# A down projection by seven block products in a one-core decoder step

## What is computed

```
n2 = rmsnorm(h, ln2);  up = n2 @ w_up              # 1024 -> 2 x 2816
u, vv = up[..., :D_FF], up[..., D_FF:]
uc, conv_tail = causal_dwconv(u, conv_prev, conv_w, conv_b)
h = h + (gelu(uc) * vv) @ w_down                   # 2816 -> 1024
y = rmsnorm(h, ln_f)
```

## Times and profile before

| | us |
|---|---|
| median of 3 runs | 885.33 (885.23 to 887.74) |
| the profiled execution | 887.28 |
| its span, first to last instruction | 885.5 |
| PE / PEld busy | 866.9 / 847.8 |
| DVE / ACT / POOL busy | 453.0 / 333.7 / 112.6 |
| granted TensorE clock, mean | 0.989 |
| moved by DMA | 81.33 MB |

### The profile page before, as it was taken

The page is one execution under the profiler, slowest core; times in us unless marked ns, Lnnn a source line. Parts: engine busy times, 40 slices in busy tenths (PEclk is TensorE's granted clock), DMA queues, the critical chain, the costliest instruction groups (busy, mean ns, idle before and its releaser), DMA issues.

```text
span 885.5 us, 16264 instructions
## 1 busy us (share of the span) xinstructions
PE 866.9 (98%) x6806; PEld 847.8 (96%) x6806; DVE 453.0 (51%) x514; ACT 333.7 (38%) x406; POOL 112.6 (13%) x171
## 2 busy tenths in 40 slices
PE   7999999999999999999999999999999999999996
PEld 7999999898889999999999999999999999999996
DVE  4554577757767444344555555555455552323322
ACT  5643243322444323222334544344434443213232
POOL 3010050511220000000000212222222210000000
PEclk9999999999999999999999999999999999999998
DMA  8431323413322222322123222222322222222202
GB/s 250 143 119 49 100 78 105 143 54 117 110 75 76 68 77 95 95 95 95 53 91 95 96 95 95 79 65 93 95 95 84 63 90 84 84 96 84 94 1 101
DMA packets 73455, 81.33 MB, mean 92 GB/s; under 512 B 2945, under 2 KB 70725, under 8 KB 73378
## 3 DMA queue, kind: packets, MB, share of 16 engines
q1 hardware_dynamic: 70468, 71.39, 25.1%
q0 software_dynamic: 2784, 8.78, 3.1%
q10 hardware_dynamic: 160, 0.53, 0.2%
HBM read 74.71 MB, written 5.97 MB: 91 GB/s over the span
## 4 chain that ended last, share of the span: by engine, by line
PE 95%; DVE 1%; ACT 1%; DMA 1%; issue 1%; SPq 0%; DVEq 0%; ACTq 0%
PE mm L1329 86%; PE ax L1337 7%; PE ax L1342 2%; DMA x_nat<-in_x_prompt 1%; DVE wlo L943 1%; DVE rstd L953 0%; ACT whi L646 0%; PE mm L1337 0%; ACT nhi L646 0%; DVE rsc L1149 0%; ACT tail_nat L646 0%; DVE rsc L1150 0%; DVE y_nat L1301 0%; ACT rstd L646 0%; ACT grs L646 0%
## 5 line engine op out<-in xcount | busy, mean ns | idle before, releaser
L1329 PE MATMUL mm<-nhi,whi 128*128 128x272 f32 x1424 | 299.6, 292 | 0.7 <-DVE wlo L943 0.6
L1329 PE MATMUL mm<-nhi,wlo 128*128 128x272 f32 x1424 | 296.1, 290 | 0.0
L1329 PE MATMUL mm<-nlo,whi 128*128 128x272 f32 x1424 | 295.6, 289 | 0.0
L1329 PEld LDWEIGHTS mm<-nhi,whi 128*128 128x128 f32 x1424 | 225.7, 190 | 3.1 <-DVE wlo L943 1.2
L1329 PEld LDWEIGHTS mm<-nlo,whi 128*128 128x128 f32 x1424 | 225.7, 190 | 0.0
L1329 PEld LDWEIGHTS mm<-nhi,wlo 128*128 128x128 f32 x1424 | 224.2, 190 | 0.0
L943 DVE TENSOR_TENSOR wlo<-raw,whi 128x2048 fp32r<-128x2048 f32 x64 | 147.8, 2310 | 107.5 <-ACT whi L646 107.4
L646 ACT ACTIVATE whi<-raw 128x2048 fp32r<-128x2048 f32 (+1 forms) x68 | 124.8, 1835 | 165.8 <-PE mm L1329 164.3
L1329 PE MATMUL mm<-ghi,whi 128*128 128x272 f32 x352 | 75.2, 289 | 0.0
L1329 PE MATMUL mm<-ghi,wlo 128*128 128x272 f32 x352 | 74.8, 288 | 0.0
L1329 PE MATMUL mm<-glo,whi 128*128 128x272 f32 x352 | 74.5, 288 | 0.0
(11 more groups left out here) (248 smaller groups left out, 945.8 us busy)
## 6 DMA issues: line engine op xcount, KB each, us to landing
raw<-in_w_in SPq DMA_DIRECT2D x44, 512.0 KB, 4.7
raw<-in_w_up SPq DMA_DIRECT2D x44, 512.0 KB, 4.1
raw<-in_w_down SPq DMA_DIRECT2D x20, 512.0 KB, 3.6
raw<-in_w_o SPq DMA_DIRECT2D x8, 512.0 KB, 3.9
x_nat<-in_x_prompt SPq DMA_DIRECT2D x4, 512.0 KB, 6.9
s0r<-in_state_ret POOLq DMA_DIRECT2D x4, 512.0 KB, 4.9
out<-s0r POOLq DMA_DIRECT2D x4, 512.0 KB, 4.1
raw<-in_w_ret_out SPq DMA_DIRECT2D x4, 512.0 KB, 3.5
```

Of the source, the lines that this page charges most:

```text
L1329: ins = pe.matmul(mm[:, 2 * j + a, 0:HALF], w, x[:, kx, HALF * a:HALF * (a + 1)], start=first and n == 0 and m == 0, stop=last and n == le ...
```

## The change

The down projection's weight matrix is seen as 2 x 2 blocks: contraction halves of 11 blocks (`KH`), output halves of 4 tiles (`MD`); the activations as 2 x 2 blocks too (contraction halves, token halves). Four block products with two contraction terms each become seven block products (Strassen) of 4 tiles, 28 parts in all. A part is 11 blocks x 3 matmuls of 128 x 272.

- Weights: a block of 128 x 11 x 128 columns comes in pieces of 512 B. Sums of weight blocks are made by transfers that POOL issues with `accum_op=ALU.add` on a buffer that holds another block: 4 `chain` buffers (three additions each, read by products 0, 2, 3 and 5) and 3 `ring` buffers (one addition in product 1, none in 4 and 6), and `first2` for one part. There are 17 plain blocks and 16 adding ones. `chain[0]` and `chain[1]` are the old `raw` slots, the other chain and the ring buffers lie at `a0`, where `nhi` and `nlo` were. Every part's weights have their own split, one part ahead.
- Activations: the up projection writes `gact` in fp32 and splits only the operand of product 0 (one half tile per round, in place of two whole tiles). POOL makes the sums for products 1, 2, 3 and 6 in place (`combine`), in pieces of 4, 4 and 3 blocks; ACT makes their high parts; DVE makes the low parts for products 1, 2, 5 and 6, POOL for 3 and 4.
- Results: DVE adds each part from PSUM to one or more quarters of `resid` (`add_part`). Squares, scaling and transposes go by halves, in an order written out in `SQUARES`.
- ACT's and DVE's lists: in step u the split of part u+2 comes first, then a piece of activations, then the rest.

The core of the diff:

```diff
+    def source(u):
+        p, m = divmod(u, MD)
+        if p in (1, 4, 6):
+            z = u - (4, 16, 24)[(1, 4, 6).index(p)] + MD * (1, 4, 6).index(p)
+            i, n = z % 3, 16 * (z // 3 + 1)
+            return ring[i], ((ring_add[i], n) if p == 1 else (ring_in[i], n))
+        if u == 2:
+            return first2, (first2_in, 16)
+        if p == 0:
+            return chain[m], (chain_in[m], 16)
+        return chain[m], (chain_add[m], 16 * (2, 3, 5).index(p) + 16)
...
+        def ring_load(z):
+            if z >= 3:
+                sp.wait_ge(lo_ready, U_DOWN + ring_part(z - 3) + 1)
+            sp.dma_start(ring[z % 3][:, :, :], block(1, 0 if 4 <= z < 8 else 1, z % MD)).then_inc(ring_in[z % 3], 16)
+        for j in range(2):
+            sp.wait_ge(filled[j], FD[j])
+        sp.dma_start(chain[3][:, :, :], block(0, 0, 3)).then_inc(chain_in[3], 16)
+        ring_load(0)
+        sp.dma_start(chain[2][:, :, :], block(0, 0, 2)).then_inc(chain_in[2], 16)
+        ring_load(1)
+        ring_load(2)
...
+        def add_block(dst, kh, mh, m, done):
+            pool.dma_start(dst[:, :, :], w_down[:, KH * kh:KH * (kh + 1), P * (MD * mh + m):P * (MD * mh + m + 1)],
+                           accum_op=ALU.add).then_inc(done, 16)
...
+        pool.wait_ge(b_lo, KH)
+        chain_step(0, 0)
+        for i in range(3):
+            combine(1, i, B_OF[2], B_OF[0], ALU.subtract)
+        chain_step(0, 1)
+        ring_step(0)
+        ring_step(1)
+        chain_step(0, 2)
+        ring_step(2)
+        for j in range(2):
+            pool.wait_ge(drained[j], FD[j])
+        combine(2, 0, B_OF[5], B_OF[2], ALU.subtract)
+        chain_step(0, 3)
+        combine(2, 1, B_OF[5], B_OF[2], ALU.subtract)
+        combine(2, 2, B_OF[5], B_OF[2], ALU.subtract)
+        ring_step(3)
+        for i in range(3):
+            pool.wait_ge(b_lo, KH + i + 1)
+            combine(3, i, B_OF[1], B_OF[5], ALU.subtract)
+        pool.wait_ge(t_ready, 9)
+        for p in (2, 3):
+            for i in range(3):
+                low_piece(p + 1, i)
+                chain_step(p, i)
+            chain_step(p, 3)
+        for i in range(3):
+            combine(6, i, B_OF[3], B_OF[4], ALU.add)
...
+        def high_part(u):
+            w, there = source(u)
+            act.wait_ge(*there)
+            act.wait_ge(part_done, u - 1)
+            run(dhi[(U_DOWN + u) % 2][:, :, :], w[:, :, :], ACT.Copy, hi_ready)
...
+        def low_part(u):
+            w, _ = source(u)
+            s = (U_DOWN + u) % 2
+            dve.wait_ge(hi_ready, U_DOWN + u + 1)
+            dve.tensor_tensor(dlo[s][:, :, :], w[:, :, :], dhi[s][:, :, :].bitcast(F32), ALU.subtract).then_inc(lo_ready, 1)
...
+        def part(u):
+            p, m = divmod(u, MD)
+            s = (U_DOWN + u) % 2
+            pe.wait_ge(lo_ready, U_DOWN + u + 1)
+            if m == 0:
+                pe.wait_ge(*LOW[p])
...
+            b = (mm, ax, ax, mm, ax, mm, mm)[p][:, m, 0:HALF]
+            for k in range(KH):
+                wh, wl, xh, xl = dhi[s][:, k, :], dlo[s][:, k, :], bhi[p % 2][:, k, :], blo[p % 2][:, k, :]
+                for n, (w, x) in enumerate(((wh, xh), (wh, xl), (wl, xh))):
+                    ins = pe.matmul(b, w, x, start=k == 0 and n == 0 and p != 3, stop=k == KH - 1 and n == 2,
+                                    skip_group_check=True)
+            ins.then_inc(part_done, 1)
```

More of the change, by code:

```diff
@@ L854, in _ @@
-        st.n += 2 * (KF // 2 - 1)
[L856 to L911, removed]
+            u = U_UP + 1
@@ L915, in last_rows @@
-            if e == 0:
-                ins.then_inc(drained_sem(name), 1)
-            else:
[L918 to L926, removed]
+            if smp is None:
+                run(*rows, ACT.Copy, drained_sem(name))
+            else:
+                st.did(act.activation(*rows, ACT.Copy))
+                run(*smp, ACT.Copy, drained_sem(name))
@@ L1260, in _ @@
-        st.off, st.n = 0, st.n + 6 * (KF // 2 - 1)
[L1262 to L1271, removed]
-                if u + 2 < U_END:
-                    lo(u + 2, u % 2, u + 3)
@@ new lines, in sums @@
+        def sums(e, sq, start, stop):
+            for j in (2 * e, 2 * e + 1):
+                small(mm[:, e, j:j + 1], sq[:, P * j:P * (j + 1)], ones[:, 0:1], start=start and j == 2 * e, stop=stop,
+                      done=last_sums if e == 0 and j == 1 else None)
+            if e == 1:
+                small(mm[0:NS, e, NJ:NJ + 1], sq[:, SEQ:NT], ones[:, 0:1], start=False, stop=stop,
+                      done=last_sums if stop else None)
+        for u in range(PARTS):
+            part(u)
+            if u == 0:
+                pe.wait_ge(ext_saved, KF)
+                turn_tail(0)
+                turn_tail(1)
+            elif u == 1:
+                turn_tail(2)
+            elif 21 <= u < 25:
+                f = u - 21
+                pe.wait_ge(fin_ready, f + 1)
+                if f == 0:
+                    pe.wait_ge(part_added, 20)
+                turn_tokens(("y", f), fin[f % 2])
+            elif u == 25:
+                turn_early(0)
+                turn_early(1)
+                pe.wait_ge(acc_done, KD + 12)
+                pe.wait_ge(part_added, 25)
+                sums(0, facc, True, True)
+            elif u == 26:
+                turn_late(4)
+                turn_late(5)
@@ L1684, in build @@
+        turn_late(6)
+        pe.wait_ge(acc_done, KD + 15)
+        pe.wait_ge(part_added, 26)
+        sums(1, facc, True, False)
+        pe.wait_ge(gap_clear, 1)
+        pe.wait_ge(last_sq, 1)
+        sums(1, osq[1], False, True)
+        turn_late(7)
     ctx.close()
```

400 lines of the change are left out of this document (276 added, 124 removed).

## The result

The changed kernel takes 908.4 us (median of four, 906.9 to 909.9) against 885.3: 2.3% slower, ratio 1.023 with an interval of 1.020 to 1.026. The forecast was 895: the sign holds, and 908.4 lies inside the range, but 23.1 us were lost where the sum said 9.7.

What follows compares the result with a forecast made beforehand. TensorE, busy 98% of the span, was taken as the bound. 887.28 - 16.5 (matmuls) + 20 (transfers) + 2 (POOL's sums) + 4 (clock) + 0.4 (tail) = 897.2, less 1.95 (profiled run to median) = 895.2, said as 895; range 869 to 920.

Steps and rivals of the forecast that it cites:

- Matmuls removed, 16.5 us: Down projection: 924 matmuls instead of 1056, 132 fewer at 0.1253 us each, takes 16.5 us off the path.
- Weight splits at 1.37 and 1.63 us: Each part's ACT copy and DVE subtraction, 3.06 us with hand-over, fit in 4.13: cost 0, cover 1.07 us.
- Transfers, 20 us: First parts of the down projection: weight transfers land late, so part 7 begins about 20 us late (15 to 22).
- Eight adding and six plain blocks: Transfers that must land before part 7: 6 x 2.24 + 8 x 4.5 = 49.4 us of all DMA engines.
- rival (a): Down projection: additions cost little more than loads; about 873 us, between 869 and 882.7; chance 0.32.
- break-even of 3.1 us per addition: Price of an adding block, 1.4 plain ones, at which the transfers ahead of part 7 use up the 16.5 us.
- Where TensorE waits: Down projection: TensorE's wait for transfers falls in three pieces, before parts 4, 6 and 7.
- Nearly none from part 8 on: Down projection: nearly no TensorE idle time from part 8 on; waits in the second half would prove the prediction wrong.
- POOL's sums, 2 us: Activation sums beside products 3 and 4 collide with DVE's own work: 2 us in all (0 to 5).
- Rival (b): Additions cheap, but POOL's list decides: part 7 at 39 us, 7 late; 883 to 888 us; chance 0.12.
- Clock, 4 us: Down projection: waits in the first eight parts lower TensorE's clock afterwards, costing 4 us (0 to 8).
- the forecast's case: Whole kernel: slower, 888 to 910 us, with an addition priced as two loads; chance 0.40.

Runs made afterwards that it cites:

- e5: e4 with each POOL transfer and ring loads 3 to 11 moving one of their 11 blocks: 870.3 us (0.980).
- e3: Changed kernel with ACT copying product 0's operand before it splits the next weights, nothing left out: 908.3 us (1.023).
- e1: Changed kernel with the 16 adding transfers made plain, same bytes, places and waits: 889.6 us (1.002).
- e4: Changed kernel with plain transfers for adding ones, activation sums cut to 2 columns per block and product 0's operand copied first: 886.5 us (0.998).
- e2: Changed kernel with POOL's twelve activation sums cut to 2 columns per block, weight additions kept: 903.6 us (1.018).
- e9: e5 with POOL's activation sums whole again: 880.8 us (0.993).
- e6: Changed kernel with each adding transfer cut to one block of 11, plain loads and sums whole: 886.0 us (0.998).
- e7: Changed kernel with 80 matmuls that nobody reads added at the end of part 3 and 66 at the end of part 6: 907.0 us (1.023).
- e8: Changed kernel with twelve single transfers, plain and adding, behind its last store; adding 512 B ones landed 8.2 and 7.7 us after issue, no kernel time given.

## Why the prediction was off, point by point

- **Matmuls removed, 16.5 us: right.** e5 shows 17.1 in the stage.
- **Weight splits at 1.37 and 1.63 us: right** (1.38 and 1.63). The cover of 1.07 us holds when neither POOL nor a transfer is in the way (e5). ACT's order in the up projection was overlooked; it makes a wait of 3.1 us that costs nothing here, because the transfers are later anyway (e3).
- **Transfers, 20 us: the step that failed.** It put part 7 at S + 51.7, and it came at S + 59.3. The price of an adding block was the disputed term, and it was nearly right: 4.0 us measured, 4.5 assumed. What was mis-sized is the plain traffic beside it. "Eight adding and six plain blocks" left out two ring loads as a term of their own (up to 4 us as a mere margin, 5.0 at the measured price), and 2.24 us per block came from rows of 1 KB, where these have 512 B and take 2.5 (1.6 more over six). And I took 20 from the middle of sums at two rates, 2.6 below what 2.24 and 4.5 give. That is 9.2 us too little, and the too high price of the additions hid 4.0 of it, by luck. With the measured numbers: the window above moved 5.14 MB at 182 GB/s and 5.47 MB at 290, 28.2 + 18.9 = 47.1 of its 47.6 us. For part 7: 8 x 4.0 + 8 x 2.5 = 52.0, 1.5 until the engines are full, 1.9 for landing, 3.1 for the splits = S + 58.5, measured S + 59.3. So part 7 is 27.6 us late instead of 20: -4.0 + 9.2 + 1.5 for the start + 0.1 for the splits, and 0.8 open. The same term is why plain transfers (e1, e4) bring nothing, where rival (a) had 873: it set fourteen blocks at 27 to 31 us, and e4 took 45 to part 7. The break-even of 3.1 us per addition was too high for the same reason: at about 2.5 (e1) the change is still 0.2% behind.
- **Where TensorE waits: half right.** Before parts 4 and 7 as said, not before 6. "Nearly none from part 8 on" doesn't hold: 4.3 us, of which 3.2 lie before parts 17 and 18, so in the second half, which the prediction named as a sign of being wrong.
- **POOL's sums, 2 us: too small as a term, missed as a bound.** Beside full DMA engines they cost 4.8 us in all (e2), of which 3.2 in product 4; that is inside the 0 to 5. Alone they cost 10.6 (e9), with part 7 at S + 38.8. Rival (b) said 39, but by luck: its sum has a last addition of 4 us, which e9 cuts to one block in eleven. With whole plain loads and small additions (e6) part 7 came at S + 44.5, and the time, 886.0, is in (b)'s range. The two bounds overlap, so neither can be read off by taking the other away: e9 + e4 would be 10.6 + 16.3 over e5, and e1, which has both, is at 19.4.
- **Clock, 4 us: in its range, by another way.** Up to part 7 it costs nothing (e7). Behind part 7 the stage takes 100.8 us against 90.6 at full pace; 4.3 are waits, about 5.9 slower matmuls: 2.9 between part 7 and part 13, behind the wait of 9.4 us (granted clock 0.74 from 797.6 to 807.0), 1.8 in part 17 behind its wait of 2.3 (0.75), the rest in small pieces. So 10.2 where I had 6 for collisions and clock together. e7 doesn't show that those 5.9 can be won: the dates of the waits at S + 87.6 and S + 107.4 didn't move when part of it was.
- **The sum.** 7.6 (transfers) + 4.2 (behind part 7) + 2.4 (ahead of the stage, run to run) - 1.0 (tail: -0.6 where I had +0.4) - 1.1 (at full pace the stage is 17.6 shorter, where I had 16.5) = 12.1. The two spans differ by 22.0, where my sum before the last subtraction says 9.9: also 12.1. The medians differ by 23.1; no term explains the other 1.1, and the runs of the changed kernel alone differ by up to 3.0.

The chances: the forecast's case was the likeliest and was the one that came, at its upper edge of 910. Three of the terms (count of blocks, rate at 512 B, waits behind part 7) were off in the same direction, and one (the price of an addition) against it, which a range for each by itself doesn't cover.

## What to carry to other kernels

When a change trades matmuls for transfers, list every transfer between the moment that buffers come free and the first part that needs the last of them, with the loads for later parts that share the engines, and price each by the rate of its own piece size; an average DMA load of a fifth says nothing of such a stretch. Then ask which dates are fixed from the start of the stage: a gain on TensorE ahead of a fixed date (e3, e7) is given back in the next wait. And when two helpers overlap, such as transfers and POOL's sums, remove both together once (e5) to see what the idea is worth, before working on either.

## What the runs showed of the hardware

- A DMA that adds to SBUF from POOL's queue moves 182 GB/s at its plateau (e8), and little else with rows of 1 KB (175) or 2 KB (200). It takes 1.91 us to issue for 11 pieces per partition; a plain one takes 1.11.
- The plain transfer of the same 704 KB from POOL's queue goes in 176 packets of 4 KB besides 16 small ones (e8); the adding one in 1408 of 512 B. SP's plain loads of such blocks went in packets of 512 B, at about 290 GB/s (e4).
- An SP ring load of 704 KB landed after 12.4 us (median up to 800 us) in the changed kernel, after 6.7 in e1_plain and 9.9 in e4_floor, where no transfer adds; the adding ring transfers took 13.1, against 8 alone (e8).
- After the wait of 11.2 us the first 24 matmuls of part 4 ran with the granted clock at its lower level, 1.2 GHz: 0.43 us for a matmul of 272 columns, spaced by 0.23, against 0.29 and 0.125. Matmuls of no use in the wait nearly prevented it (0.78 to 1.00 in the stretch up to part 7, e7), and gained nothing.
